# A second adaLN modulation computed beside the Mamba projections: its products moved from TensorE to ScalarE, its sums to GpSimd

## The reference, cut to what matters

```
def modulation(cvec, w, b):
    return jnp.split(jax.nn.silu(cvec) @ w + b, 6, axis=-1)
...
mx = modulation(c, ada_w[i], ada_b[i])
mc = modulation(c_ctx, ada_w[i], ada_b[i])
```

## Time and profile before

| | |
|---|---|
| median of three runs | 2203.14 us |
| the profiled execution, its own time | 2207.39 us |
| its span in the profile | 2205.9 us |
| TensorE matmul busy | 2034.8 us, 92% |
| VectorE busy | 1051.5 us, 48% |
| ScalarE busy | 501.9 us, 23% |
| GpSimd busy | 154.1 us, 7% |
| mean granted TensorE clock | 0.97 of full speed |
| stage 2, groups 0 to 7 | about 120 to 1002 us |

### The profile page before, as it was taken

The page is one execution under the profiler, slowest core; times in us unless marked ns, Lnnn a source line. Parts: engine busy times, 40 slices in busy tenths (PEclk is TensorE's granted clock), DMA queues, the critical chain, the costliest instruction groups (busy, mean ns, idle before and its releaser), DMA issues.

```text
span 2205.9 us, 28385 instructions
## 1 busy us (share of the span) xinstructions
PE 2034.8 (92%) x10602; PEld 1219.1 (55%) x10602; DVE 1051.5 (48%) x1743; ACT 501.9 (23%) x593; POOL 154.1 (7%) x214
## 2 busy tenths in 40 slices
PE   5789999999999999998999799988989889898888
PEld 2367777777777777776778533333333333333333
DVE  2454666666666666666785623333222333322224
ACT  3132333333333333334444300000000000000000
POOL 0000010101010101010592100000000000000000
PEclk9799999999999999999999899999999999999999
DMA  9967676767666767668663699999999999999996
GB/s 352 312 218 230 186 216 186 213 186 213 186 213 185 215 186 214 187 214 273 216 221 115 261 425 427 426 427 427 425 427 426 425 427 428 425 426 426 426 425 271
DMA packets 294718, 666.69 MB, mean 302 GB/s; under 512 B 13504, under 2 KB 188000, under 8 KB 261008
## 3 DMA queue, kind: packets, MB, share of 16 engines
q1 hardware_dynamic: 285728, 639.45, 77.9%
q0 software_dynamic: 7984, 26.40, 3.1%
q10 hardware_dynamic: 960, 0.23, 0.1%
HBM read 655.40 MB, written 10.65 MB: 302 GB/s over the span
## 4 chain that ended last, share of the span: by engine, by line
DMA 28%; PE 17%; POOL 4%; DVE 1%; issue 1%; SPq 1%; ACT 0%; DVEq 0%; POOLq 0%
DMA wt<-in_moe_w_up 28%; PE bank L1827 12%; PE bank L1682 2%; POOL ysq L635 1%; POOL ysq L642 1%; POOL ysq L640 1%; PE bank L1852 1%; SPq L526 1%; PE bank L1791 0%; PE bank L1792 0%; PE bank L1809 0%; PE bank L1743 0%; PE bank L1736 0%; PE bank L1784 0%; DVE x L1450 0%
## 5 line engine op out<-in xcount | busy, mean ns | idle before, releaser
L1827 PE MATMUL bank<-wt,xe 128*64 128x512 f32 x1984 | 467.9, 627 | 82.7 <-DMA wt<-in_moe_w_up 82.7
L1450 DVE TENSOR_TENSOR x<-x,bank 128x512 f32<-128x512 f32 x256 | 158.4, 681 | 538.2 <-PE bank L1809 538.2
L1570 PE MATMUL bank<-hTh,whi 128*128 128x256 f32 (+1 forms) x1264 | 406.7, 342 | 1.2 <-DVE dtw L1112 1.2
L1571 PE MATMUL bank<-hTl,whi 128*128 128x256 f32 (+1 forms) x1264 | 398.9, 336 | 0.0
L1827 PEld LDWEIGHTS bank<-wt,xe 128*64 128x64 f32 x1984 | 164.8, 144 | 382.6 <-issue 382.6
L1570 PEld LDWEIGHTS bank<-hTh,whi 128*128 128x128 f32 x1264 | 240.0, 190 | 80.5 <-issue 56.2
L1571 PEld LDWEIGHTS bank<-hTl,whi 128*128 128x128 f32 x1264 | 240.2, 190 | 23.4
L1575 PE MATMUL bank<-hTh,wlo 128*128 128x256 f32 (+1 forms) x1264 | 231.1, 335 | 0.0
L1852 PE MATMUL bank<-wt,hdn 128*64 128x512 f32 x1024 | 226.8, 595 | 1.4 <-DVE hdn L1462 1.4
L960 DVE TENSOR_TENSOR wlo<-raw,whi 128x2048 fp32r<-128x2048 f32 x80 | 183.2, 2290 | 86.6 <-ACT whi L703 86.2
L1575 PEld LDWEIGHTS bank<-hTh,wlo 128*128 128x128 f32 x1264 | 196.8, 190 | 24.3
(11 more groups left out here) (305 smaller groups left out, 1877.6 us busy)
## 6 DMA issues: line engine op xcount, KB each, us to landing
wt<-in_moe_w_gate SPq DMA_DIRECT2D x64, 2048.0 KB, 16.7
wt<-in_moe_w_up SPq DMA_DIRECT2D x64, 2048.0 KB, 21.1
wt<-in_moe_w_down SPq DMA_DIRECT2D x64, 2048.0 KB, 18.6
raw<-in_ssm_w_in SPq DMA_DIRECT2D x80, 1024.0 KB, 6.1
raw<-in_ada_w SPq DMA_DIRECT2D x70, 1024.0 KB, 5.2
raw<-in_ssm_w_out SPq DMA_DIRECT2D x32, 1024.0 KB, 5.2
fr<-in_ada_w SPq DMA_DIRECT2D x26, 1024.0 KB, 12.2
bc<-cum_d POOLq DMA_DIRECT2D x32, 512.0 KB, 7.3
```

Of the source, the lines that this page charges most:

```text
L1450: dve.tensor_tensor(x1[:, tt, cols], x1[:, tt, cols], banks[(1, 3, 6, 7)[nb]][:, :], ALU.add).then_inc(s_acc2, 1)
L1570: pe.matmul(bank[:, 0:width], wh[:, k, :], hTh[:, k, 0:width], start=(k == 0), stop=False)
L1571: last = pe.matmul(bank[:, 0:width], wh[:, k, :], hTl[:, k, 0:width], start=False, stop=False)
L1827: last = pe.matmul(banks[0][SLOTS * h:SLOTS * h + SLOTS, :], rows[:, k, :], wt[2 * q + h][:, FF * i:FF * i + FF], start=(k == 0), stop=(k ...
```

## The change

ScalarE multiplies each of the four 128 x 512 parts of a tile in place by its column of `cvec`, at the end of the same steps as before. GpSimd adds the four products: parts 0 and 1 plus parts 2 and 3 in one instruction of 1024 elements per partition, then the two halves (512), then that to the running sum `arow` (512; the first tile of four writes `arow` directly and saves this one). TensorE no longer reads the tiles. It sums `arow` over the partitions with a column of ones, twice per group as before, now in steps 5 and 9. A ring slot of a tile is free when GpSimd has added it. GpSimd's queue gets the adds between its loads and stores, and `y_stores` is cut in two. ScalarE's copy of `ADAK` to `arow` is gone.

```
+ADDS = [2, 5, 8, 11, 13, 16, 19, 22]
+NADD = ADDS[-1]
...
-                    for i in range(4):
-                        sp.wait_ge(s_ada[i], NADA * bg + (ADA1 + n + 1))
+                    sp.wait_ge(s_aadd, NADD * bg + ADDS[n])
...
+            def ada_adds(g, j):
+
+                done = NADD * g + (ADDS[j - 1] if j else 0)
+                tile = a_view(raw_of(POS[("a", j)]))
+                pool.wait_ge(s_aprod, NADA * g + (j + 1))
+                pool.tensor_tensor(tile[:, 0:2, :], tile[:, 0:2, :], tile[:, 2:4, :], ALU.add).then_inc(s_aadd, 1)
+                pool.wait_ge(s_aadd, done + 1)
+                if j % 4 == 0:
+                    if not (isinstance(g, int) and g == 0 and j == 0):
+                        pool.wait_ge(s_asum, 2 * g + j // 4)
+                    pool.tensor_tensor(arow[:, :], tile[:, 0, :], tile[:, 1, :], ALU.add).then_inc(s_aadd, 1)
+                else:
+                    pool.tensor_tensor(tile[:, 0, :], tile[:, 0, :], tile[:, 1, :], ALU.add).then_inc(s_aadd, 1)
+                    pool.wait_ge(s_aadd, done + 2)
+                    pool.tensor_tensor(arow[:, :], arow[:, :], tile[:, 0, :], ALU.add).then_inc(s_aadd, 1)
+
+            for j in range(4):
+                ada_adds(0, j)
             pool.wait_ge(s_cumr, 1)
...
             load_bc(0, 0)
+            for j in range(4, NADA):
+                ada_adds(0, j)
             with pool.Fori(0, GROUPS - 1) as s:
+                ada_adds(s + 1, 0)
                 bc_other_half(s)
-                y_stores(s)
+                for j in range(1, 4):
+                    ada_adds(s + 1, j)
+                y_stores(s, (0, 1))
                 pool.wait_ge(s_seg, 2 * s + 2)
                 pool.wait_ge(s_ebc, 2 * s + 2)
                 load_bc(s + 1, 0)
+                for j in range(4, 6):
+                    ada_adds(s + 1, j)
+                y_stores(s, (2, 3))
+                for j in range(6, NADA):
+                    ada_adds(s + 1, j)
...
-                    if w and n in (4, 9):
-                        ada_row(g, n // 9)
...
-            def ada_row(g, j):
-
+                    if w and n in ADA_STEP:
+                        ada_products(g, ADA_STEP[n])
+
+            def ada_products(g, j):
+
+                pos = POS[("a", j)]
+                act.wait_ge(s_raw[raw_of(pos)], raw_count(group_raw(g), pos))
+                tile = a_view(raw_of(pos))
                 for i in range(4):
-                    act.wait_ge(s_ada[i], NADA * g + (ADA1 + 4 * j + 4))
-                if not (isinstance(g, int) and g == 0 and j == 0):
-                    act.wait_ge(s_asum, 2 * g + j)
-                act.activation(arow[:, :], ADAK[:, :], ACT.Copy).then_inc(s_adaev, 1)
+                    k = 4 * (j % 4) + i
+                    last = act.activation(tile[:, i, :], tile[:, i, :], ACT.Copy, scale=cvec[:, k, 0:1])
+                last.then_inc(s_aprod, 1)
...
-                    pe.matmul(ADAK[32 * i:32 * i + 2, :], cvec[:, 4 * (j % 4) + i, :], a_view(raw_of(pos))[:, i, :],
-                              start=(j % 4 == 0), stop=(j % 4 == 3), tile_position=(0, 32 * i)).then_inc(s_ada[i], 1)
-
-            def ada_columns(g, j):
-
-                pe.wait_ge(s_adaev, 2 * g + (j + 1))
-                for i in range(4):
-                    last = pe.matmul(ADAC[:, 8 * j + 2 * i:8 * j + 2 * i + 2], arow[:, P * i:P * i + P], sel[:, :], start=True, stop=True)
+                    last = pe.matmul(ADAC[:, 8 * j + 2 * i:8 * j + 2 * i + 1], arow[:, P * i:P * i + P], ones[:, 0:1], start=True, stop=True)
                 last.then_inc(s_asum, 1)
...
-                    if w and n in ADA_STEP:
-                        ada_tile_sum(g, ADA_STEP[n])
-                    if w and n in (4, 9):
+                    if w and n in (5, 9):
                         ada_columns(g, n // 9)
```

More of the change, by code:

```diff
@@ L336, in build @@
         s_asum = sem("s_asum")
-        s_adaev = sem("s_adaev")
+        s_aprod = sem("s_aprod")
+        s_aadd = sem("s_aadd")
         s_ads = sem("s_ads")
@@ L499, in _ @@
                     else:
-                        for c in range(4):
-                            sp.wait_ge(s_ada[c], NADA * (GROUPS - 1) + ADA1 + bn + 1)
+                        sp.wait_ge(s_aadd, NADD * (GROUPS - 1) + ADDS[bn])
                 else:
@@ L602, in bc_other_half, with y_stores @@
                 load_bc(s, 1)
-            def y_stores(s):
-                for c in range(GC):
+            def y_stores(s, chunks=range(GC)):
+                for c in chunks:
                     pool.wait_ge(s_yout, GC * s + c + 1)
@@ L1182, in steps @@
                         differences(s, 1)
-                    if w and n == 4:
+                    if w and n == 6:
                         ada_columns(g, 0)
@@ L1644, in c_times_b, with ada_columns @@
                 last.then_inc(s_cb, 1)
[L1646 to L1654, removed]
-                for i in range(4):
-                    pe.matmul(ADAK[32 * i:32 * i + 2, :], cvec[:, 4 * (j % 4) + i, :], a_view(raw_of(pos))[:, i, :],
-                              start=(j % 4 == 0), stop=(j % 4 == 3), tile_position=(0, 32 * i)).then_inc(s_ada[i], 1)
-            def ada_columns(g, j):
-                pe.wait_ge(s_adaev, 2 * g + (j + 1))
-                for i in range(4):
-                    last = pe.matmul(ADAC[:, 8 * j + 2 * i:8 * j + 2 * i + 2], arow[:, P * i:P * i + P], sel[:, :], start=True, stop=True)
+            def ada_columns(g, j):
+                pe.wait_ge(s_aadd, NADD * g + ADDS[4 * j + 3])
+                if isinstance(g, int) and g == 0 and j == 0:
+                    pe.wait_ge(s_azero, 1)
+                else:
+                    pe.wait_ge(s_ads, 2 * g + j)
+                for i in range(4):
+                    last = pe.matmul(ADAC[:, 8 * j + 2 * i:8 * j + 2 * i + 1], arow[:, P * i:P * i + P], ones[:, 0:1], start=True, stop=True)
                 last.then_inc(s_asum, 1)
```

## The result

The kernel after takes 2294.43 us (median of four runs, 2290.48 to 2294.85); the kernel before, run beside it, 2204.1. The ratio is 1.0397, 95% interval 1.0382 to 1.0412: slower by 4.0%. The forecast was 2269 us, with a range to 2295.

What follows compares the result with a forecast made beforehand. TensorE sets the pace, with VectorE's chain to the states equally long. Seven groups at +8.2 us (+57) and group 0 at +9 give +66 on 2207.4, 2273; the median, 4.3 lower, is 2269 us, range 2204 to 2295.

Steps and rivals of the forecast that it cites:

- ScalarE, +2.5 on A: From a group's end to the states: tile 0's products delay `whi` of chunk 2, moving the states by 2.5 us.
- The port in A, +4.9: Before the states: GpSimd's adds block VectorE for whole instructions, 1.6 us by tile 0 and 3.3 by tile 1.
- A as a whole, 39.7: Stretch from a group's end to the states: 39.7 us in place of 32.3.
- The clock, +1.7: After some 8 us idle before the states, TensorE restarts at 1.2 GHz: 1.7 us more per group.
- B, 14.3: Stretch from the states to the end of the first y chunks: 0.97 us shorter, 14.3 us.
- C, 29.0: First to second y chunks: 29.0 us in place of 26.1, through late w5, blocked VectorE and `ce`.
- D, 33.9: Stretch from the second y chunks to the next group's end: 2.9 us shorter, 33.9 us.
- Group 0, +9: First group, without a scan: late products and weight requests, with one clock fall, cost 9 us.
- (a): Rival: GpSimd's adds cost VectorE nearly nothing; period 109.5 us, total 2206 us; chance 0.12.
- (b): Rival: faster, products don't push `whi`, adds cost nothing; seven groups of -5.8 us, total 2155 us; chance 0.10.
- (c): Rival: late ring slots become the bound once a tile's adds take over 8 us; total 2302 us; chance 0.10.
- (d): Rival: `ada_columns` waits in TensorE's queue for GpSimd's sums, room 2 us in step 9; chance counted within (c).

Runs made afterwards that it cites:

- better order: Kernel after with adds cut to 4 to 8 elements, and ScalarE multiplying tile 0 behind `whi` of chunk 2 instead of ahead: period 105.96 us.
- tiny adds: Kernel after with GpSimd's adds cut to 4 to 8 elements, ScalarE's products and all waits kept: period 108.6 us.
- late ring without long adds: Kernel after with adds of 4 to 8 elements, and SyncE passing 2 or 3 small DMAs before freeing a slot: period 108.6 us.
- port only: Kernel after with full-size GpSimd adds reading `hTh`, slots released by ScalarE's products, sums wrong: period 122.8 us.
- the pieces: Kernel after with every GpSimd add cut into instructions of 256 elements, all computed: 2307.36 us, ratio 1.0463.
- half version: Tiles 0 to 3 as in the kernel before, 4 to 7 the new way: 2196.8 us; with tile 6's adds ahead of the y stores, 2182.48 us.
- first kernel with memsets: Kernel after with adds of 4 to 8 elements, each behind one-element GpSimd memsets lasting 0.8 us where 2.2 were meant: period 108.3 us.

## Why the prediction was right, and where its sizes were off

The forecast was slower by the port, VectorE's chain and the clock, and that is what happened. The parts of a period, each from the table: TensorE's relief, with ScalarE in the better order, 110.27 to 105.96, -4.3; ScalarE's order 105.96 to 108.57, +2.6; adds of tiles 0 and 1 to 114.90, +6.3; adds of the others to 120.02, +5.1.

- **ScalarE, +2.5 on A**: +2.45 (tiny adds).
- **The port in A, +4.9**: 6.3. The mechanism was right, and tile 0's share nearly: 1.6 forecast, 0.38 + 1.09 measured on `wlo` and `store`. The step that failed is tile 1's: 3.3 forecast, 4.86 measured. I charged turns to instructions with two SBUF inputs and to `differences`, and let the third add run under the drain. But the copy of `bT` and the `tensor_scalar` behind it, with one input, gave two turns (2.7 and 1.1 us), so the third add met `weights` (1.1 us) and none was left for the drain. `scaled_x`, whose means were to grow, kept 1.22 us: no add reached it. The Trainium skill ("SBUF — State Buffer", Who interferes with whom) says that a VectorE copy, cast or `tensor_scalar` can run in a mode that takes the shared port pair, and then blocks or is blocked for a whole instruction; the copy at 868.06 (2.97 us against 0.29 with tiny adds) and the cast at 901.71 (2.38 against 0.30) agree.
- **A as a whole, 39.7**: 41.7 on average, 41.4 in the group shown. Beside the 1.4 us of turns there is a term that the forecast put at nothing: the ring makes the next group's first weights late, since tile 6's slot is released behind its adds. Chunk 1's `wlo` starts 3.7 us behind the group's end in place of 3.0, in single groups 5.2. The late ring without long adds shows the same (3.8), full adds of tiles 0 and 1 alone do not (3.0). So 32.2 + 2.45 + 6.3 + 0.7 = 41.7.
- **The clock, +1.7**: the states took 3.75 us in place of 1.98, 1.8 more.
- **B, 14.3 and C, 29.0**: from the states to the end of the first y chunks (900.53) 15.9 us, which with the clock's 1.7 is the forecast, and from there to y2 28.8. The wait for chunk 5, forecast at 2.6 us, is 2.80. The exponentials begin 1.84 us behind `whi` of chunk 5, released by `differences`, as the forecast has it; the blocked `ce` (4.50 us) is the one turn of tile 4's first add. From y1 to y2 the kernel after needs 4.7 us more than with tiny adds, where I had 29.0 - 24.1 = 4.9.
- **D, 33.9**: 33.6 from y2 to the end.
- **Group 0, +9**: +12.1. The late ring is the main cause. With tiny adds the group ends at 226.0, 3.8 us before that of the kernel before, so full adds cost it 15.9 us; a ring late by two or three small DMAs brings back 12.2 of them, the adds without a late ring (port only) 1.4. Chunk 3 starts at 169.7, even before the 172 of the forecast, but behind it TensorE waits for weights twice more, 4.62 us for chunk 5 (at 188.76) and 3.27 us for chunk 8 (at 218.37); the forecast named only chunk 5.
- **Stages behind, 0**: +2.6, not looked into. And I took the median as 4.3 below the profiled execution, as before; here it lies 3.95 above. That is a third of the 25 us by which I was low: 8.2, beside 11 from the periods, 3 from group 0 and 2.6 from behind.

**The rivals.** (a), a free port: the period would be 109.5; it is so only with tiny adds (108.6). (b), faster: with tiny adds in the better order the period does fall by 4.3 us, less than the 5.8 that I gave it, which already left TensorE's savings in A out: A is 0.7 longer than before, and the states take some 3.5 us at the lower clock in place of 1.98. (c), the ring as the bound: in groups 1 to 7 of the kernel after it costs the 0.7 us in A and nothing else that these runs show. A late ring alone leaves the period as it is with tile 2's slot 4.6 us behind its products and costs 18 us per group at 11.8; I had put the turning point at over 8. How much of the kernel's 4.7 us from y1 to y2 the ring would cost without the port, at its own 7.5 us, stays open: the delays tried lie on either side. The port alone costs all of it. (d), a wait for GpSimd's sums: TensorE's list of waits for groups 1 to 7 has none.

## What to carry to other kernels

An engine's low share of busy time does not make it free: here GpSimd's adds were paid by VectorE, one whole instruction per turn (6.3 us in A), and copies and casts paid as well as additions. Before moving work off the engine that seems to be the bound, find the stretches where its neighbour's chain is as long as its own work, and move only the rest: four tiles moved gained 1.1%, eight lost 4.0%. Put the release of a buffer ahead of work in the queue that waits for something else (1.3 us of A in the half version). And cut a stretch at a point where two causes part, as at chunk 1's `wlo` here: the mean of A alone hid that the pieces had made the turns cheaper.

## What the runs showed of the hardware that was not expected

- VectorE's one-input instructions are blocked by GpSimd's adds: a copy of 128x256 takes 2.97 us beside an add of 1024 elements, 0.64 beside one of 256, 0.29 with none.
- Sixteen `tensor_scalar` take 7.39 us beside one-element memsets of GpSimd (34 ns each) and 3.76 without, while two-input `weights` keep 3.42. The same section of the Trainium skill has it that VectorE's two-input instructions contend only with a GpSimd instruction that reads SBUF, and names no such condition for its two-port modes; these rows agree with both.
- The length of a wait alone does not tell whether TensorE's clock falls behind it. With waits of 8.3 us and more ahead of the states it was down in all seven groups of the kernel after (3.64 to 3.78 us for them). With 3.4 to 3.5 us it was down in six of seven groups with tiny adds (3.48 to 3.78 us; 2.40 in the seventh), but behind the same waits in the first kernel with memsets the states took 1.98 us in two groups. With 1.9 us in the half version it fell in two groups (3.7 us) and not in three others (1.98 us). And in the kernel after a wait of 1.78 us (ahead of 863.60) was enough: granted clock 0.57 from 866.00 to 868.00.
